# GpSimd makes the low half of each weight unit in four operations of 256 columns instead of one of 1024

## The reference

```python
for l in range(2):                                   # first block
    proj = rms_norm(x, attn_norm[l]) @ w_in[l]       # then three attentions on slices of proj
    x = x + concat([rms_norm(mla), diff, rms_norm(chunk)]) @ w_out[l]
    h = conv3(rms_norm(x, ffn_norm[l]) @ w_ffn_in[l])
    x = x + (silu(g) * u) @ w_ffn_out[l]             # u, g = split(h), 2816 wide each
x = rms_norm(x, final_norm)
for l in range(2):                                   # second block
    proj = x @ w_in_2[l]                             # banded and dilated attention, gates
    x = layer_norm(a * x + (ga * (oa @ w_a) + gb * (ob @ w_b)) @ w_out_2[l])
    mlp = relu(x @ w_up[l]) ** 2 @ w_down[l]         # 4096 wide
    ple = sigmoid(x @ w_ple_gate[l] + b) * (p[l] @ w_ple[l])
    x = layer_norm(a * x + mlp + ple)
```

## Time and profile before

| what | us |
|---|---|
| median of 3 runs | 2972.64 (2964.82 to 2974.21) |
| the profiled execution's own time | 2969.5 |
| its span in the profile | 2967.8 |
| TensorE busy | 2912.6 (98%) |
| VectorE busy | 1384.4 (47%) |
| GpSimd busy | 1364.0 (46%) |
| ScalarE busy | 839.7 (28%) |

### The profile page before, as it was taken

How to read it: one execution, slowest core, us unless ns; L and a number is a source line. 1 busy time by engine, 2 the same in 40 slices (tenths; PEclk the granted TensorE clock), 3 DMA queues, 4 the chain that set the end, 5 groups by cost and what they waited for, 6 DMA issues and landing times.

```text
span 2967.8 us, 40808 instructions
## 1 busy us (share of the span) xinstructions
PE 2912.6 (98%) x14054; PEld 2400.3 (81%) x14054; DVE 1384.4 (47%) x3151; ACT 839.7 (28%) x1881; POOL 1364.0 (46%) x924
## 2 busy tenths in 40 slices
PE   7999999999999999999999999999999999999998
PEld 6778888888778888879888878888798888788886
DVE  6476525265476524344774541112547744411124
ACT  3354312122363212121553230011225532300112
POOL 4222555564313555555233645555453336455553
PEclk9999999999999999999999999999999999999999
DMA  7323666665324666666343756666563337566663
GB/s 254 107 78 108 191 192 191 194 213 167 107 79 132 188 194 185 199 197 198 101 128 118 223 169 192 191 195 194 158 196 110 121 117 224 167 194 189 196 192 111
DMA packets 136521, 494.16 MB, mean 167 GB/s; under 512 B 15280, under 2 KB 15536, under 8 KB 136112
## 3 DMA queue, kind: packets, MB, share of 16 engines
q0 software_dynamic: 66240, 241.20, 26.7%
q1 hardware_dynamic: 68544, 245.40, 26.2%
q10 hardware_dynamic: 1584, 5.46, 0.5%
HBM read 489.91 MB, written 2.10 MB: 166 GB/s over the span
## 4 chain that ended last, share of the span: by engine, by line
PE 94%; DVE 2%; ACT 2%; issue 1%; DMA 1%; POOL 0%; SPq 0%; POOLq 0%; DVEq 0%; ACTq 0%
PE ps L558 26%; PE ps L560 25%; PE ps L559 25%; PE ps L744 3%; PE ps L767 2%; PE ps L815 2%; PE ps L693 1%; PE ps L694 1%; PE ps L695 1%; PE ps L757 1%; PE ps L807 1%; PE ps L796 1%; PE ps L797 1%; DVE lo L1146 1%; PE ps L1038 0%
## 5 line engine op out<-in xcount | busy, mean ns | idle before, releaser
L558 PE MATMUL ps<-hi,w_hi 128*128 128x512 f32 x3216 | 1273.1, 396 | 10.1 <-DVE lo L1603 5.4
L560 PE MATMUL ps<-lo,w_hi 128*128 128x512 f32 x3216 | 1257.8, 391 | 0.0
L559 PE MATMUL ps<-hi,w_lo 128*128 128x512 f32 x3216 | 1257.5, 391 | 0.0
L531 POOL TENSOR_TENSOR w_lo<-w_raw,w_hi 128x1024 fp32r<-128x1024 f32 x460 | 1106.2, 2405 | 103.0 <-DMA w_hi<-weights 93.8
L526 POOL DMA_DIRECT2D w_hi<-weights x460 | 261.9, 569 | 1466.3 <-PE ps L560 1352.4
L558 PEld LDWEIGHTS ps<-hi,w_hi 128*128 128x128 f32 x3216 | 607.5, 189 | 160.6 <-issue 29.6
L560 PEld LDWEIGHTS ps<-lo,w_hi 128*128 128x128 f32 x3216 | 606.5, 189 | 128.7
L559 PEld LDWEIGHTS ps<-hi,w_lo 128*128 128x128 f32 x3216 | 607.6, 189 | 119.5 <-issue 1.0
L1993 ACT ACTIVATE ps<-hb,col 128x512 f32<-128x512 f32 x88 | 68.6, 782 | 381.1 <-DVE hb L1173 381.1
L1746 DVE SCALAR_TENSOR_TENSOR x<-x,ps 128x512 f32<-128x512 f32 x64 | 43.9, 687 | 256.7 <-PE ps L560 256.7
L1173 DVE TENSOR_TENSOR hb<-ps,rx 128x512 f32<-128x512 f32 x88 | 60.1, 686 | 187.3 <-PE ps L560 174.3
(11 more groups left out here) (345 smaller groups left out, 3256.2 us busy)
## 6 DMA issues: line engine op xcount, KB each, us to landing
w_raw<-weights SPq DMA_DIRECT2D x460, 512.0 KB, 3.5
w_hi<-weights POOLq DMA_DIRECT2D x460, 512.0 KB, 3.9
x<-xt SPq DMA_DIRECT2D x8, 256.0 KB, 10.2
out<-x SPq DMA_DIRECT2D x8, 256.0 KB, 2.0
kc<-k ACTq DMA_DIRECT2D x1, 1346.0 KB, 5.6
bias<-relb ACTq DMA_DIRECT2D x2, 512.0 KB, 5.0
bias<-relb ACTq DMA_DIRECT2D x1, 1024.0 KB, 4.9
praw<-pt ACTq DMA_DIRECT2D x2, 512.0 KB, 6.1
```

The costliest lines, as they stand in the source:

```text
L531: nc.gpsimd.tensor_tensor(wlo[s][:, :], raw[s][:, :], whi[s][:, :].bitcast(F32), ALU.subtract).then_inc(w_split, 1)
L558: nc.tensor.matmul(out_ap, w[0], xx[0], start=first, stop=False)
L559: nc.tensor.matmul(out_ap, w[1], xx[0], start=False, stop=False)
L560: return nc.tensor.matmul(out_ap, w[0], xx[1], start=False, stop=last)
```

## The change

The single subtraction over 1024 columns becomes four over 256 columns each, on the same tensors. The waits ahead are the same two, and the semaphore is raised once, by the last of the four. Nothing else is different.

```diff
             def low_half(s, i):
                 pool.wait_ge(w_loaded[s], i * 16 + 16)
                 pool.wait_ge(w_hi_in[s], i * 16 + 16)
-                nc.gpsimd.tensor_tensor(wlo[s][:, :], raw[s][:, :], whi[s][:, :].bitcast(F32),
-                                        ALU.subtract).then_inc(w_split, 1)
+                for k in range(4):
+                    w = slice(k * UNIT // 4, (k + 1) * UNIT // 4)
+                    last = nc.gpsimd.tensor_tensor(wlo[s][:, w], raw[s][:, w], whi[s][:, w].bitcast(F32), ALU.subtract)
+                last.then_inc(w_split, 1)
```

## The result

The changed kernel takes 2978.7 us (median of 12 runs), the kernel before beside it 2972.4 us (12 runs): a ratio of 1.0028 (95% interval 1.0019 to 1.0037). The medians are 6.3 us apart, the ratio makes 8.3 us: slower, where 8.6 us faster were forecast.

A forecast was written before the change was run, and what follows sets the result against it. TensorE, busy 2912.6 of 2967.8 us, was taken as the bound. Added GpSimd time of +3.8 us and VectorE's gain of -12.4 us gave -8.6 us, median 2964.0; forecast's own range 2958 to 2968, 8 in 10 2957 to 2984.

The forecast's parts named there:

- the condition of the whole gain: VectorE's blocked operations wait at most 0.8 us, if the port is given between pieces; together -12.4 us.
- The term of -4.2 us at 669.30: After eight blocks ending layer 0: TensorE's 2.55 us wait and the slow-clock stretch behind it go, -4.2 us.
- rival A: GpSimd keeps the port over all four pieces: +15 us, 2988; with cheap pieces +5, 2978. Chance 0.30, half dear, half cheap.
- Duration of a piece: GpSimd's low-half unit: 0.3 us fixed per added piece, 3.3 us a unit; 0.83 us a piece.
- The start: At the very start, TensorE waits directly for the first two splits: +0.9 us.
- 30.96 and 47.81 (-5.1): Start phase: wait at 30.96 goes (-1.4), wait at 47.81 falls to 0.72 (-2.5), low clock behind it -1.2; sum -5.1 us.
- rival B: Port released but nothing moves: ScalarE's table loads late at 47.81, GpSimd at 669.30; -2.8 us, 2969.8. Chance 0.15.
- +1.5 us: Layer 0's 6-block groups: GpSimd 0.1 to 0.2 us late per unit, plus VectorE's port turns; +1.5 us.
- 1734.84 and layer 1 (-2.6): At 1734.84 and the same place in layer 1: L1603's shorter block gives -1.3 us each, -2.6.
- The attention stages, counted at -0.5: Blocked operations inside the attention stages have TensorE's other products beside them; counted at -0.5 us.
- C: Pieces are dear, 4.1 us a unit or more, while the port is released: +1.6 us, 2974. Chance 0.08.
- What would show it: Signs in the profile: L1146's mean falls from 2048 to 1000-1300 ns in the forecast, rises above 2300 in rival A.

The follow-up runs named there:

- open breaks in every unit: Against the kernel before: four pieces in all units, with GpSimd waiting for its own piece's end before starting the next; ratio 1.0019.
- the memsets: Against the kernel before: the whole subtraction kept, then twelve one-column memsets into a spare tile, signal on the last; ratio 1.0029.
- open breaks and the first three units whole: Against the kernel before: four pieces with GpSimd waiting between them, but the first three and the 32 six-block units whole; ratio 0.9982.
- the tiny operations: Against the kernel before: the whole subtraction kept, then three 4-column subtractions into a spare tile, signal on the last; ratio 1.0014.

## Why the prediction was wrong

Two steps failed. The first is the condition of the whole gain, "if the port is given to it between pieces" (-12.4 us). It is mostly not: 14 of 21 blocked L1148 stood through all four pieces. The second doesn't hang on the port. The term of -4.2 us at 669.30 took VectorE for the only late link, where GpSimd's own unit was but 1.4 us ahead of the restart; the wait grew from 2.55 to 4.88 us although VectorE was done 4.1 us ahead. With open breaks in every unit the time was still 1.0019 of before.

The number of rival A in its cheap form (pieces of 0.1 us more each, +5 us, 2978 us) came almost exactly, 2978.7, but that is in part luck. Its mechanism was a chain of VectorE of 5.0 us a block; what came was a faster VectorE and a late GpSimd there, and the memsets give the same loss with the port left as it was. In the second block the rival is right in kind (0.4 us more at 1733, where it had 0.9).

Point by point:

- *Duration of a piece.* Taken as 0.3 us per added piece, 3.3 us a unit; measured 2.82 us, 0.14 us per added piece. Mis-sized by half, on the safe side.
- *The start.* +0.9 us was forecast for the directly waited-for units, +1.6 us measured, and it does not reach the end of the start stage.
- *30.96 and 47.81 (-5.1).* With held pieces the start is 1.7 us shorter, by the openings that it happened to get, in one execution and 2.3 us longer in another kernel. With open breaks and the first three units whole it is 5.1 us shorter, with open breaks in all units 2.2: the size was right for the first, the condition was not met.
- *669.30 (-4.2).* Wrong in either case. With open breaks throughout the stage grew by 7.3 us, with pieces by 2.9. The releaser in the earlier trace rows was VectorE, but GpSimd's own unit came out at 667.89, and the forecast named no successor here (rival B did). It had the period right ("GpSimd works without a pause and waits for landings") and priced it in the same part at +1.5 us, then subtracted the wait as if VectorE alone set it. Whole operations under otherwise open breaks still wait 1.96 us for GpSimd.
- *1734.84 and layer 1 (-2.6).* With open breaks everywhere 1.3 us a layer, as forecast; with held pieces L1605 takes 3.53 us at 1729.80 instead of 3.14, and the wait 1.32 instead of 0.91: the sign turned over. The attention stages, counted at -0.5, cost 0.4 us in the wait at 1554 (2.30, before 1.91) and 0.4 in the one at 1562 (0.53, before 0.12). These and the wait at 1733 make up nearly all of the 1.3 us of layer 2.0. Here the held port is the cause: the three waits are 2.30, 0.51 to 0.53 and 1.29 to 1.32 us in all four kernels with four held pieces in this layer, and 1.92 to 1.93, 0.12 to 0.14 and 0.91, as before, in the two where GpSimd's unit is as long but the subtraction is whole.
- *The other rivals.* C fell: the pieces are cheap. B was right in kind at 669.30, where GpSimd is the late link, and wrong at 47.81, where the wait did go to 0.72 us once the breaks were open.
- *What would show it.* L1146 at 1000 to 1300 ns meant the forecast, above 2300 rival A; 1774 was between them, since the port opens at some breaks. The bound for A, 3.3 us held every time, was as wrong as the forecast's 0.5 us wait.

The Trainium skill's sentence that the port pair is locked for a whole instruction (SBUF — State Buffer, "SBUF: two separate sides") holds for the end of the lock, 0.56 us before VectorE's end as measured over whole operations; read as "four pieces are four locks" it misled: the L1148 at 637.63 stood through four. The Trainium skill's sentence that a GpSimd core goes on without a join (GPSIMD Engine Reference, section 2.1) fits that row, and the 0.04 us by which the pieces overlap. It does not explain the tiny operations, which follow just as closely and were overtaken.

What stays open: which breaks open by themselves. It isn't length alone (four columns yes, 512 mostly no), nor the order alone. It isn't mere chance either: in the kernel with eight pieces the blocked operation ends 3.51 to 3.53 or 3.10 to 3.11 us after the first piece in eight units, and the two values come as a pair at 276, 645 and 936 us. Nothing was run to find what decides it. It stays open, too, why three changes that add the same 0.4 us a unit cost 1.0014, 1.0028 and 1.0029. How the loss of 1.0028 divides between GpSimd's lateness in the six-block stage (about 3 us) and the second block (1 to 3 us a layer, where the longer stand of VectorE shows in the waits at 1554, 1562 and 1733) is known only within those bounds; the three waits alone are 1.2 us in layer 2.0, and low-clock stretches of 2 us fall differently in each execution.

## What to carry to other kernels

In this kernel, cutting an operation of GpSimd into pieces that follow at once mostly did not hand the shared port to VectorE; a wait of GpSimd for its own piece does, and it costs GpSimd 0.13 us per break (3.20 against 2.82 us a unit) and some 0.3 to 0.5 us per opening. Put such breaks only where VectorE's chain is late and GpSimd has slack (here 12 of 460 units gave all of the gain), and leave the operation whole where GpSimd itself is the next late link. Before taking a wait off the sum, look up the end time of every other thing that the waiting instruction needs, not only of the releaser that the profile names: at 669.30 the second one, GpSimd's unit, came only 1.2 us ahead of VectorE's residual.

## What the runs showed of the hardware that was not expected

- Four GpSimd subtractions that follow at once mostly keep VectorE out (14 of 21), so that its operation ends 0.56 us after the last one's end, as with one; at some breaks VectorE gets in, and the GpSimd unit is 0.45 us longer for it (2.82, 3.27, 3.75 us with none, one, two).
- Behind another operation an added 256-column piece costs 0.14 us, a 4-column subtraction 0.15 us, a one-column memset some 0.03 us of GpSimd's time (0.40 us for twelve).
- Tiny subtractions behind a whole one let VectorE in first (0.93 us for three instead of 0.44).
- The stage from 62.7 to 231 us, in which TensorE's work is the same in all kernels, took 164.5 us at a mean granted clock of 1.00 and 168.3 at 0.97.
